# Order of work at the entry of attention, a wide triangle for the gates' sums, and the order of ScalarE's copies in the second block's attention

## The reference

```
h = rms_norm(x, attn_norm[l])
proj = h @ w_in[l]
(fq, fk, fv, ff, dq, dk, dv, sq, sk, sv, iq, ik, iw) = split(proj)
log_f = log_sigmoid(ff + fox_fb[l]);  cum_logf = cumsum(log_f, axis=1)
o_fox  = softmax(rms_norm(fq) . rms_norm(fk) * scale + cum[t] - cum[s], causal) @ fv   # 6 heads
o_diff = (softmax(q1 . k1) - lam * softmax(q2 . k2)) @ dv                              # 4 heads
score  = sum_h iw[t, h] * relu(iq[t, h] . ik[s] * idx_scale);  keep the 128 best keys
o_dsa  = softmax(sq . sk over the kept keys) @ sv                                      # 6 heads
x = x + concat(o_fox, o_diff, o_dsa) @ w_out[l]
x = x + (silu(gate) * up) @ w_down[l]          # gate, up = rms_norm(x) @ w_gate_up[l]
```

```
p = softmax(concat(q.k_band * scale + mask, q.k_ctx * scale, sink));  o = p_loc @ v + p_ctx @ v_ctx
p = softmax((qn.kn + qr.kr) * scale over context and latent keys);    o = p @ v
p = softmax(concat(q.k_rows * scale + bias[h], q.k_ctx * scale));     o = p_loc @ v + p_ctx @ v_ctx
y = (o * silu(z)) @ out_w
```

## Time and profile before

| | |
|---|---|
| median of 3 runs | 2447.67 us (2444.7 to 2449.34) |
| profiled execution | 2443.78 us |
| its span | 2441.9 us |
| TensorE busy | 2301.8 us, 94% |
| its weight load | 1854.1 us, 76% |
| VectorE busy | 1262.2 us, 52% |
| ScalarE busy | 928.6 us, 38% |
| GpSimd busy | 258.2 us, 11% |
| TensorE's share of the chain that ended last | 52% |

### The profile page before, as it was taken

One profiled execution on the slowest core, in us unless ns is written; L12 is line 12 of the kernel. 1 busy time (PEld: TensorE's weight loads), 2 busy tenths in 40 slices (PEclk: granted clock), 3 DMA queues, 4 the chain that ended last, 5 costly groups with the idle time before them and its releaser, 6 DMA issues.

```text
span 2441.9 us, 32031 instructions
## 1 busy us (share of the span) xinstructions
PE 2301.8 (94%) x13033; PEld 1854.1 (76%) x13033; DVE 1262.2 (52%) x1836; ACT 928.6 (38%) x1555; POOL 258.2 (11%) x167
## 2 busy tenths in 40 slices
PE   6989899999999988999999999998998989999988
PEld 6776578888888765688888878896676878876666
DVE  4577448963225578359853254225555352225654
ACT  3436643222224355642222231324544232125553
POOL 2001112121001001122121000000000000002210
PEclk9989999999999988999999999999999999999999
DMA  4210015532223110035523311320000233222311
GB/s 150 82 65 1 1 52 190 189 121 87 104 96 100 61 35 1 14 125 173 188 88 103 105 62 54 104 88 31 18 10 14 70 99 106 69 71 40 59 25 52
DMA packets 144611, 189.46 MB, mean 78 GB/s; under 512 B 41141, under 2 KB 94402, under 8 KB 144450
## 3 DMA queue, kind: packets, MB, share of 16 engines
q1 hardware_dynamic: 108816, 168.26, 21.2%
q10 hardware_dynamic: 35586, 19.01, 3.4%
q0 software_dynamic: 64, 0.16, 0.0%
HBM read 179.94 MB, written 7.47 MB: 77 GB/s over the span
## 4 chain that ended last, share of the span: by engine, by line
PE 52%; DVE 6%; ACT 3%; issue 2%; ACTq 1%; DMA 0%; POOL 0%; DVEq 0%; POOLq 0%
PE ps L481 36%; PE ps L1707 5%; PE ps L1731 3%; PE ps L1745 2%; ACT probs L1797 1%; PE ps L2217 1%; DVE probs_t L1915 1%; PE ps L2246 1%; PE ps L2234 1%; PE ps L1687 1%; DVE ps L1885 1%; DVE score L2103 1%; DVE neg_max L1866 1%; DVE top L2100 1%; PE ps L669 0%
## 5 line engine op out<-in xcount | busy, mean ns | idle before, releaser
L457 DVE TENSOR_TENSOR w_low<-w_raw,w_high 128x2048 fp32r<-128x2048 f32 (+4 forms) x140 | 305.4, 2181 | 537.0 <-ACT w_high L452 537.0
L452 ACT ACTIVATE w_high<-w_raw 128x2048 fp32r<-128x2048 f32 (+4 forms) x140 | 252.8, 1806 | 613.3 <-PE ps L481 599.8
L481 PE MATMUL ps<-h_hi,w_high 128*128 128x512 f32 x976 | 372.3, 381 | 3.4 <-DVE h_lo L2594 3.2
L481 PE MATMUL ps<-h_lo,w_high 128*128 128x512 f32 x976 | 370.0, 379 | 0.0
L481 PE MATMUL ps<-h_hi,w_low 128*128 128x512 f32 x976 | 369.7, 379 | 0.0
L481 PE MATMUL ps<-w_high,h_hi 128*128 128x512 f32 (+3 forms) x736 | 279.4, 380 | 9.8 <-DVE w_low L457 6.4
L481 PE MATMUL ps<-w_high,h_lo 128*128 128x512 f32 (+3 forms) x736 | 276.6, 376 | 0.0
L481 PE MATMUL ps<-w_low,h_hi 128*128 128x512 f32 (+3 forms) x736 | 276.4, 376 | 0.0
L481 PEld LDWEIGHTS ps<-h_hi,w_high 128*128 128x128 f32 x976 | 184.3, 189 | 38.6 <-issue 4.1
L481 PEld LDWEIGHTS ps<-h_hi,w_low 128*128 128x128 f32 x976 | 184.1, 189 | 34.9
L481 PEld LDWEIGHTS ps<-h_lo,w_high 128*128 128x128 f32 x976 | 184.3, 189 | 34.4 <-issue 0.5
(11 more groups left out here) (314 smaller groups left out, 3621.6 us busy)
## 6 DMA issues: line engine op xcount, KB each, us to landing
w_raw<-in_w_gate_up SPq DMA_DIRECT2D x44, 1024.0 KB, 5.1
ada_w<-in_ada_w SPq DMA_DIRECT2D x24, 1024.0 KB, 5.2
w_raw<-in_w_down SPq DMA_DIRECT2D x20, 1024.0 KB, 4.9
w_raw<-in_w_in SPq DMA_DIRECT2D x16, 1024.0 KB, 5.0
w_raw<-in_c_in_w SPq DMA_DIRECT2D x16, 1024.0 KB, 5.5
w_raw<-in_w_out SPq DMA_DIRECT2D x8, 1024.0 KB, 4.9
w_raw<-in_ab_in_w SPq DMA_DIRECT2D x8, 1024.0 KB, 5.1
bias<-bias_scratch ACTq DMA_DIRECT2D x32, 224.0 KB, 4.9
```

Of the source, the lines that this page charges most:

```text
L452: e.activation(w_high[j % 2][:, 0:size], w_raw[j % 2][:, 0:size], ACT.Copy).then_inc(sig.w_high_done, 1)
L457: e.tensor_tensor(w_low[j % 2][:, 0:size], w_raw[j % 2][:, 0:size], w_high[j % 2][:, 0:size].bitcast(F32), ALU.subtract).then_inc(sig.w_lo ...
L481: mm = e.matmul(dst, lhs, rhs, start=start and a == 0, stop=stop and a == 2)
```

## The change

Four edits. `square` of part i - 2 now follows the second piece's high part in groups 2 to 5, in place of ending groups 1 to 4. In the last group VectorE empties its banks ahead of the low part of the out-projection's weights. The gates' sums use one wide tile, a triangle followed by 384 columns of ones, and one product per j over all columns from tile j on. In `WidePairs` ScalarE copies the turned part ahead of the exps in both attentions, and the unit's output behind them.

```diff
+        tri_wide = at("tri_wide", [P, S], F32, PJ_END + 16384 + 6144)
@@ sum_gates
-                for t in range(NT):
-                    for j in range(t + 1):
-                        mm = e.matmul(ps[0:70, 7, t * P:(t + 1) * P], small[:, 640 + j * 70:640 + (j + 1) * 70],
-                                      cst("tri") if j == t else ones[:], start=j == 0, stop=j == t)
+                for j in range(NT):
+                    mm = e.matmul(ps[0:70, 7, j * P:S], small[:, 640 + j * 70:640 + (j + 1) * 70], tri_wide[:, 0:S - j * P],
+                                  start=j == 0, stop=j == NT - 1)
@@ InProduct.scalar
                     if i:
                         first_piece(b, i, odd)
+                    if 2 <= i <= 5:
+                        self.square(e, B, i - 2)
...
-                    if 1 <= i <= 4:
-                        self.square(e, B, i - 1)
@@ prepare (VectorE, group 1)
+                ch.step(e.memset(tri_wide[:, P:S], 1.0))
+                ch.step(e.tensor_copy(tri_wide[:, 0:P], cst("tri")))
@@ InProduct.vector
-                    size = self.next_size if i == self.groups - 1 else self.kts[0] * self.columns(i + 1)
-                    cut_low(e, b, self.pieces + odd, size)
+                    if i == self.groups - 1:
+                        self.evac.vector(e, b, L, self, i, ch)
+                        cut_low(e, b, self.pieces + odd, self.next_size)
+                        continue
+                    cut_low(e, b, self.pieces + odd, self.kts[0] * self.columns(i + 1))
@@ WidePairs.scalar
-                    if s in self.mid and not self.grid:
+                    if s in self.mid:
                         copy_turned(self.mid[s], 7)
+                    if s + 1 < self.N:
+                        exps(s + 1)
                     if s - 1 in self.ends:
                         copy_o(self.ends[s - 1])
-                    if s + 1 < self.N:
-                        exps(s + 1)
-                    if s in self.mid and self.grid:
-                        copy_turned(self.mid[s], 7)
```

## The result

The changed kernel takes 2417.12 us (median of 4 runs, 2412.66 to 2420.48), beside 2446.18 for the kernel before on the same chip: a ratio of 0.9883, with a 95% interval of 0.9855 to 0.9911. My number was 2421, in a range of 2408 to 2437. The profiled execution took 2414.55 us, with a span of 2412.9, which is 29.0 less than before.

A forecast was written before the change was run, and what follows sets the result against it. TensorE, busy 94% of the span, was taken as the bound, so savings had to come from its idle time or clock. 7.0 + 9.6 + 0 + 3.0 + 6.8 = 26.4 us saved gave 2421 us, range 2408 to 2437.

The forecast's parts named there:

- Gates: First block's gates: splitting weights ahead of squares ends a TensorE wait and low clock; 3.5 us a layer, 7.0 together.
- Entry, the wait: End of in-projection, two layers: split and value copies first cut TensorE's wait from 4.74 to 0.85 us, 3.9 a layer.
- Entry, the clock: Start of first block's attention: clock still falls, but after the eight turns, saving 0.9 us a layer.
- Rival B: Start of first block's attention: TensorE stays at 2.4 GHz, 8.2 us less in two layers, 2413; chance 0.19.
- Triangle: Gates' sums: four wide products for ten, same 1280 columns; no gain, bounds -1.8 and +1.1 us a layer.
- First attention of block two: Output copies behind exps save 1.5 us at three sinks and 1.5 at the end; 3.0, bounds 0 and 4.
- the exps no longer wait for the values, which brings the sink 0.5 us ahead: Second block's first attention: the sink comes 0.5 us sooner at three places, 1.5 us in all.
- Grid: Grid attention: turned copies ahead of exps save 1.0 us seven times, VectorE late next; net 6.8, bounds 3 and 10.
- D: Grid attention: copying turned parts first delays TensorE's next turning of probabilities at 21 copies; slower, 2463; chance 0.04.
- E: Whole kernel: waits only change hands to other readers, time within 4.9 us of before, 2445; chance 0.06.
- C: Waits go but clock doesn't follow: gates give back 3.4 us, attention's low stretches grow 3 a layer; 2431, chance 0.19.

The follow-up runs named there:

- a_between: On the changed kernel, in grid attention VectorE copies its bank of turned probabilities between the two heads' maxima instead of behind them; 2407.34 us.

## Why the prediction was right, step by step

The sum was closer than its terms. Against the forecast the entry's clock gave 4.2 us more and the grid 1.2, and the second block's first attention 3.5 less. That these misses nearly cancel is luck; the waits at the gates, at the entry and in the grid are what was foreseen.

**Gates.** Right in mechanism and size: 3.7 us a layer, forecast 3.5. The split of wait and clock was off by little: 2.2 and 1.55, where I had 1.8 and 1.7. What I had taken for certain, that the clock falls behind this wait, happens in 8 of 10 places.

**Entry, the wait.** Right: 3.9 saved a layer, the wait 0.86 where I had 0.85, and the mask's copy ends 2.6 us sooner where I had 2.7. The two single edits left waits of 2.10 and 2.51, so the edits share the gain: 2.6 for the earlier chain, 2.2 for the low part, and 3.9 and not 4.8 together, because behind 0.86 stands the copy's own time.

**Entry, the clock.** This is the term that was mis-sized. I took 0.9 us a layer and measured 3.0; the low stretch did not keep its length behind the turnings, it shrank from 13.6 to 3.4 us. That it is the clock shows in the entries of other kernels: with a low stretch of 10.2 us this part takes 20.5 to 20.9 us in four entries of three kernels with different edits, and with none 17.5 to 17.6 us in seven. Rival B had the right direction but also the wrong price: the clock does fall (in seven of eight entries), and what is left of it costs 0.5 to 0.6 us a layer, not the half of 8.2. Waits of 4.7, 2.5, 2.1 and 0.86 us were followed by low stretches of 13.6 to 27, 10.2 and 13.7, 10.2 twice, and mostly 3.4. The order is loose: behind 0.86 there were also 10.2 and 20.5 in two of eight entries, and the kernel before with its filled gaps had 20.5 and 6.8 behind 4.7. The page that the forecast named for rival B (TensorE: Matmul & The Clock Gate, of the Trainium skill) has a rule that long idle gaps bring the clock down. The runs agree for the long wait, and show besides that three gaps of 0.86, 0.69 and 0.69 us go with a fall, and filling two of them with none.

**Triangle.** Right: 2.07 against 2.10 us.

**First attention of block two.** Half wrong. The last wait for exps went (from 1.61 to nothing listed, 1.4 us saved). The step "the exps no longer wait for the values, which brings the sink 0.5 us ahead" failed: the sink's exp was ahead, but it was not what VectorE's sum waited for. I had read the releaser that the wait named, and not GpSimd's product beside it. Each of four sinks comes 0.15 us later instead, 0.6 in all. The rest of the stage's -0.5 is the clock, a low stretch of 6.8 us at 1643 in place of 3.4, worth 1.3.

**Grid.** Right: the new bound is VectorE's copy with 0.5 of waiting, and a_between showed it by removing it. The six middle units gave 5.9, for which I had 6.0. The first unit gave 2.1 where I had 0.8. Of that, 0.85 is the biases' transfers, which took ScalarE's queue 4.0 us to issue before and 3.2 after; over all kernels this took 3.0 to 4.0 us, whatever the order. With it taken off, the first unit is 24.5 to 24.8 us long in the five kernels with the new order and VectorE's copy in its old place, and 25.4 to 25.7 in the five with the old order: about 0.9 belongs to the change, and the last 0.3 is not explained. Rivals D and E had no part: a step takes 5.5 us with no wait for exps, and the listed waits of the six middle units fell from 12.2 to 6.6 us in all. Of C's kind is only the low stretch at 1643.

By these steps the change is worth 7.5 and 7.7 us, 6.0 of clock, 1.4, -0.6 and 6.8: 28.8 of the 29.0 us. The rest are differences of both signs at places that also move in kernels that do not touch them, as the program's start (0.7) and the end of the span (-1.1). What stays open is which stretches the clock falls in, and why it stays low for 7, 14, 20 or 27 us behind equal waits.

## What to carry to other kernels

Follow a late engine's queue back to the one instruction that stands ahead of the needed one and could stand behind it; nearly all of the 29 us came from such swaps, with no instruction of the slow engines saved. When a short VectorE instruction lasts several times its usual time, look at what GpSimd does beside it before trusting the named releaser. When a wait is cut, say what is late next and by how much: in the grid that named the following edit, which made that stage 9 us shorter again.

## What the runs showed of the hardware that I had not expected

A VectorE addition of 128x4 with two SBUF inputs took 1.24 us beside a GpSimd product and 0.16 alone, and ended within 0.03 us of it. The same wait of 1.45 us on TensorE was followed by 3.4 us at a granted clock of 0.50 in 8 of 10 places and by none in 2. With constants turned for 0.6 us in each of two or three idle gaps of TensorE, the low stretch behind the entry's wait of 0.86 was gone in six of six places (it stood in seven of eight without). Behind the wait of 4.7 it stayed, 20.5 and 6.8 us long, yet that kernel ran 12.3 us faster, at a mean granted clock of 0.978 to 0.981 in place of 0.971 to 0.974.
